# A two-block transformer on one core: four edits to the order of ACT, DVE and POOL, and scores of the compressed keys with the keys as weights

## The reference, cut to what matters

```python
h = x                                              # first block
h = h + moba_nsa_mixer(rmsnorm(h, mix_norm[0]))    # "even": 8 MoBA heads, 8 NSA heads
h = h + sqrelu_mlp(rmsnorm(h, mlp_norm[0]))        # "mlp0"
h = h + fox_mixer(rmsnorm(h, mix_norm[1]))         # "fox"
h = h + sqrelu_mlp(rmsnorm(h, mlp_norm[1]))        # "mlp1"
h = rmsnorm(h, final_norm)                         # the first block's last norm
# second block: n = rmsnorm(h) * g * (1 + scale) + shift, added back times a gate
h = h + 0.5 * gt1 * swiglu(n1)                     # "glu0"
h = h + gt2 * hybrid_mixer(n2)                     # "dil": pooling and dilated attention
h = h + 0.5 * gt3 * swiglu(n3)                     # "glu1"
out = rmsnorm(h, g_final)
```

```python
s_cmp = einsum('gjqd,gnd->gjqn', qn, k_cmp) * scale + bias
p_cmp = masked_softmax(s_cmp, d_cmp >= 0)
o_cmp = einsum('gjqn,gnd->gjqd', p_cmp, v_cmp)
```

## Time and profile before

| | us |
|---|---|
| median of 3 runs (lowest, highest) | 1099.05 (1098.44, 1100.7) |
| the profiled execution | 1098.95 |
| its span, first to last instruction | 1097.2 |
| busy in it: PE / PEld / DVE / ACT / POOL | 1076.2 / 918.3 / 778.6 / 660.4 / 115.5 |
| mean granted clock of PE | 0.996 |

### The profile page before, as it was taken

One profiled execution on the slowest core, in us unless ns is written; L12 is line 12 of the kernel. 1 busy time (PEld: TensorE's weight loads), 2 busy tenths in 40 slices (PEclk: granted clock), 3 DMA queues, 4 the chain that ended last, 5 costly groups with the idle time before them and its releaser, 6 DMA issues.

```text
span 1097.2 us, 15918 instructions
## 1 busy us (share of the span) xinstructions
PE 1076.2 (98%) x6098; PEld 918.3 (84%) x6098; DVE 778.6 (71%) x1261; ACT 660.4 (60%) x1067; POOL 115.5 (11%) x209
## 2 busy tenths in 40 slices
PE   8999999999999999999999999999999999999997
PEld 7898788888888998888888788888878978888885
DVE  6767667777786776687676777887875766565566
ACT  6667676565666776766565754354475766444443
POOL 2033101010100531020000000110000200000000
PEclk9999999999999999999999999999999999999999
DMA  9842348878864643687778467768545344555551
GB/s 341 298 158 79 115 156 326 304 289 306 300 217 173 212 140 113 217 306 279 255 277 312 154 227 289 294 244 312 188 165 183 131 154 173 192 191 183 185 183 64
DMA packets 40619, 238.30 MB, mean 217 GB/s; under 512 B 4661, under 2 KB 5845, under 8 KB 17632
## 3 DMA queue, kind: packets, MB, share of 16 engines
q1 hardware_dynamic: 26784, 188.81, 48.3%
q0 software_dynamic: 13040, 47.85, 11.7%
q10 hardware_dynamic: 720, 0.62, 0.2%
HBM read 236.15 MB, written 1.11 MB: 216 GB/s over the span
## 4 chain that ended last, share of the span: by engine, by line
PE 81%; DVE 9%; ACT 5%; issue 3%; DMA 1%; POOL 0%; DVEq 0%; ACTq 0%
PE bank L1570 20%; PE bank L1539 13%; PE bank L1541 13%; PE bank L1540 13%; PE bank L1571 10%; PE bank L1694 2%; DVE w_lo L1070 2%; PE bank L1758 1%; ACT w_hi L699 1%; PE bank L1740 1%; DVE ada_raw L1300 1%; PE bank L1732 1%; PE bank L1588 1%; PE bank L1589 1%; PE bank L1592 1%
## 5 line engine op out<-in xcount | busy, mean ns | idle before, releaser
L1570 PE MATMUL bank<-a_two,w_hi 128*128 128x512 f32 x1088 | 386.9, 399 | 0.8 <-DVE w_lo L1070 0.8
L1070 DVE TENSOR_TENSOR w_lo<-raw,w_hi 128x2048 fp32r<-128x2048 f32 x122 | 278.4, 2303 | 107.2 <-ACT w_hi L699 107.1
L1571 PE MATMUL bank<-a_two,w_lo 128*128 128x256 f32 x1088 | 305.5, 281 | 0.0
L699 ACT ACTIVATE w_hi<-raw 128x2048 fp32r<-128x2048 f32 x122 | 232.2, 1910 | 63.5 <-DMA raw<-in_stream 63.4
L1570 PEld LDWEIGHTS bank<-a_two,w_hi 128*128 128x128 f32 x1088 | 204.5, 188 | 51.0 <-issue 1.4
L1571 PEld LDWEIGHTS bank<-a_two,w_lo 128*128 128x128 f32 x1088 | 205.7, 189 | 1.7
L1539 PE MATMUL bank<-w_lo,hid_hi 128*128 128x512 f32 x432 | 169.6, 393 | 0.3 <-DVE w_lo L1070 0.2
L1540 PE MATMUL bank<-w_hi,hid_lo 128*128 128x512 f32 x432 | 168.7, 390 | 0.0
L1541 PE MATMUL bank<-w_hi,hid_hi 128*128 128x512 f32 x432 | 168.6, 390 | 0.0
L871 ACT ACTIVATE cross<-bank 128x256 f32<-128x256 f32 x136 | 51.5, 381 | 186.2 <-PE bank L1571 186.1
L1059 DVE TENSOR_TENSOR w_lo<-raw,w_hi 128x1024 fp32r<-128x1024 f32 x104 | 125.5, 1229 | 22.3 <-ACT w_hi L688 22.2
(11 more groups left out here) (231 smaller groups left out, 1478.4 us busy)
## 6 DMA issues: line engine op xcount, KB each, us to landing
raw<-in_stream SPq DMA_DIRECT2D x173, 1024.0 KB, 5.0
ada_raw<-in_ada POOLq DMA_DIRECT2D x72, 512.0 KB, 5.3
cmpw<-in_stream SPq DMA_DIRECT2D x4, 1024.0 KB, 8.1
rel_band<-rel_scratch POOLq DMA_DIRECT2D x2, 1024.0 KB, 7.2
cum_row<-cum_scratch POOLq DMA_DIRECT2D x4, 512.0 KB, 4.8
gate_row<-gate_scratch POOLq DMA_DIRECT2D x3, 512.0 KB, 5.8
h<-in_x SPq DMA_DIRECT2D x2, 512.0 KB, 4.3
raw<-in_stream SPq DMA_DIRECT2D x2, 512.0 KB, 7.0
```

Of the source, the lines that this page charges most:

```text
L699: nc.scalar.activation(w_hi[:, u % RING, :], raw[:, u % RING, :], ACT.Copy).then_inc(hi_ready, 2)
L1070: nc.vector.tensor_tensor(w_lo[:, u % RING, :], raw[:, u % RING, :], w_hi[:, u % RING, :].bitcast(F32), ALU.subtract).then_inc(lo_ready, 2)
L1570: nc.tensor.matmul(ps[bank][:, 0:2 * T], wh[:, k, cols_], a_two[:, :, k, :], start=k == 0, stop=False)
L1571: ins = nc.tensor.matmul(ps[bank][:, T:2 * T], wl[:, k, cols_], a_hi[:, k, :], start=False, stop=k == KT - 1)
```

## The change

- ACT, at the start: chunk 3 of both tiles and two halves of unit 3 are done before the copy of `rrow`. DVE's order there is not changed.
- POOL, at the start: the first zeroes wait until DVE has done six halves of `w_lo`.
- Even mixer: the scores of the compressed keys are made with `kc` as weights (128 x 32) and the queries of both token tiles (256 columns) as what moves, in plain fp32. The four heads of a group write to four groups of 32 partitions of bank 2. This is done one tick earlier, in km0/0. ACT copies the bank to the new buffer `score_rows`, and in km0/1 PE turns it with four transposes back to the layout that DVE reads.
- The turns `gmix` and `gf2` get a function of their own on ACT and DVE, `gated_turn`. ACT takes tile 1's root before chunk 3 of tile 0 and before the half unit. DVE shifts chunk 1 before chunk 0's low part, adds tile 1's second half before it shifts chunk 3, adds epsilon right after that, and makes the inverse before chunk 3's low part.
- glu0: the two halves of each tile of the first block's last norm are scaled in steps j and j + 1, not both in j.

```diff
@@ -263,6 +263,7 @@
 
         par = place("par", [P, N_COLS])
         kc = place("kc", [P, 2, 2, 16], F32R)
+        score_rows = place("score_rows", [P, 2, T])
         vcmp = place("vcmp", [16, 2, HD])
         four_rows = place("four_rows", [P, 32])
         hidc = place("hidc", [P, 2, 2, 32])
@@ -601,6 +604,7 @@
             pool.dma_start(rpick[:, :], rel_pick).then_inc(pick_landed, 16)
             pool.dma_start(bfor[:, :], b_forget).then_inc(bfor_landed, 16)
             pool.wait_ge(pool_step, 1)
+            pool.wait_ge(lo_ready, 6)
             zeros(slice(0, 6), 0)
             pool.wait_ge(rel_rows_sb, 1)
             pool.dma_start(rel_dram[:, 0:REL], rrow[:, :]).then_inc(rel_stored, 16)
@@ -764,6 +768,21 @@
                 inv = fin[:, t, 12:13] if name == "gf1" else stat[:, 7, t:t + 1]
                 for c0, c1 in ((0, 256), (256, 512), (512, 1024)):
                     nc.scalar.activation(tok[:, t, c0:c1], h[:, t, c0:c1], ACT.Copy, scale=inv).then_inc(rows_scaled_act, 1)
+
+            def gated_turn(name, gain, shift):
+
+                squares(name, 0)
+                round_half()
+                scale(name, 0)
+                turned(name, 0, gain, shift, (0, 1))
+                square_half(name, 1, 0)
+                turned(name, 0, gain, shift, (2,))
+                square_half(name, 1, 1)
+                root(name, 1)
+                turned(name, 0, gain, shift, (3,))
+                round_half()
+                scale(name, 1)
+                turned(name, 1, gain, shift)
 
             def norm_turn(name, gain, shift=None):
 
@@ -935,10 +954,12 @@
                 turned("mix0", t, gain0, chunks=(2,))
             round_half()
             round_half()
+            for t in range(TT):
+                turned("mix0", t, gain0, chunks=(3,))
+            round_half()
+            round_half()
             act.wait_ge(rel_rows, 1)
             nc.scalar.activation(rrow[:, :], ps[4][0:16, 0:REL], ACT.Copy).then_inc(rel_rows_sb, 1)
-            for t in range(TT):
-                turned("mix0", t, gain0, chunks=(3,))
             advance(FIRST["v_even"] + 4)
 
             def even_extras(tick):
@@ -963,6 +984,9 @@
                     act.wait_ge(ck_done, 1)
                     nc.scalar.activation(kc[:, :, 0, 0:15], ps[2][:, 0:32].rearrange("p (g n) -> p g n", g=2)[:, :, 0:15],
                                          ACT.Copy).then_inc(kc_hi, 1)
+                if tick.at("km0", 0, 0):
+                    act.wait_ge(crows, 1)
+                    nc.scalar.activation(score_rows[:, :, :], ps[2][:, :].rearrange("p (g t) -> p g t", g=2), ACT.Copy).then_inc(crows_sb, 1)
                 if tick.at("km1", 0, 0):
                     act.wait_ge(cshifted, 1)
                     nc.scalar.activation(pc[:, :, 0:15], pc[:, :, 0:15], ACT.Exp, scale=-1.0).then_inc(cprobs, 1)
@@ -998,7 +1022,7 @@
             act.wait_ge(gain_ready, 2)
             norm_turn("gf1", gainc[:, 0:KT], modc[:, 0:KT])
             glu("glu0")
-            norm_turn("gmix", gainc[:, KT:2 * KT], modc[:, 3 * KT:4 * KT])
+            gated_turn("gmix", gainc[:, KT:2 * KT], modc[:, 3 * KT:4 * KT])
             advance(FIRST["uv_dil"] + 4)
 
             def dil_extras(tick):
@@ -1025,7 +1049,7 @@
 
             mixer("dil", DIL_TICKS, dil_extras)
             act.wait_ge(gain_ready, 3)
-            norm_turn("gf2", gainc[:, 2 * KT:3 * KT], modc[:, 6 * KT:7 * KT])
+            gated_turn("gf2", gainc[:, 2 * KT:3 * KT], modc[:, 6 * KT:7 * KT])
             glu("glu1")
             for t in range(TT):
                 squares("last", t)
@@ -1086,12 +1110,16 @@
                     chain(nc.vector.tensor_tensor(tok[:, t, half], ps[bank][:, :], gate[:, half], ALU.mult))
                     nc.vector.tensor_tensor(to, to, tok[:, t, half], ALU.add).then_inc(h_ready, 1)
 
-            def inverse_root(name, t):
-
+            def first_mean(name, t):
+
+                dve.wait_ge(sumsq, squares_before(name, t) + 1)
+                nc.vector.tensor_scalar(stat[:, 2, t:t + 1], stat[:, 0, t:t + 1], EPS[name], None, ALU.add).then_inc(mean_ready, 1)
+
+            def inverse_root(name, t, first_taken=False):
                 n = NORM[name]
                 first, v, y, b = (stat[:, i, t:t + 1] for i in (2, 4, 5, 6))
-                dve.wait_ge(sumsq, squares_before(name, t) + 1)
-                nc.vector.tensor_scalar(first, stat[:, 0, t:t + 1], EPS[name], None, ALU.add).then_inc(mean_ready, 1)
+                if not first_taken:
+                    first_mean(name, t)
                 dve.wait_ge(mean_ready, n + t + 1)
                 dve.wait_ge(sumsq, squares_before(name, t) + 2)
                 chain(nc.vector.tensor_scalar(v, stat[:, 1, t:t + 1], first, -0.5, ALU.add, ALU.mult))
@@ -1150,20 +1178,23 @@
                 polish(t, 9, 11, 14, 15)
                 chain(nc.vector.scalar_tensor_tensor(out=f[:, 13:14], in0=f[:, 15:16], scalar=1.5, in1=f[:, 14:15], op0=ALU.add, op1=ALU.mult))
 
-            def turned(name, t, gain, shift=None, chunks=(0, 1, 2, 3)):
+            def shift_chunk(name, t, c, gain, shift):
 
                 m = TURN[name] + 4 * t
+                dve.wait_ge(bank_turned, m + c + 1)
+                if t == 1:
+                    dve.wait_ge(act_split, m - 4 + c + 1)
+                for kt in (2 * c, 2 * c + 1):
+                    ins = nc.vector.tensor_scalar(shifted[:, c, kt % 2, :], ps[TURN_BANKS[name][t][c]][:, (kt % 2) * P:(kt % 2 + 1) * P],
+                                                  gain[:, kt:kt + 1], shift[:, kt:kt + 1], ALU.mult, ALU.add)
+                ins.then_inc(rows_shifted, 1)
+
+            def turned(name, t, gain, shift=None, chunks=(0, 1, 2, 3), shifts=True):
+
                 ts = slice(t * P, (t + 1) * P)
                 for c in chunks:
-                    if shift is not None and c < 2:
-                        odd = 2 * c + 1
-                        dve.wait_ge(bank_turned, m + odd + 1)
-                        if t == 1:
-                            dve.wait_ge(act_split, m - 4 + odd + 1)
-                        for kt in (2 * odd, 2 * odd + 1):
-                            ins = nc.vector.tensor_scalar(shifted[:, odd, kt % 2, :], ps[TURN_BANKS[name][t][odd]][:, (kt % 2) * P:(kt % 2 + 1) * P],
-                                                          gain[:, kt:kt + 1], shift[:, kt:kt + 1], ALU.mult, ALU.add)
-                        ins.then_inc(rows_shifted, 1)
+                    if shift is not None and c < 2 and shifts:
+                        shift_chunk(name, t, 2 * c + 1, gain, shift)
                     dve.wait_ge(act_high, split_no(name, t, c))
                     bank, c0 = turned_at(name, t, c)
                     if shift is not None:
@@ -1177,6 +1208,24 @@
                                 out=a_lo[:, kt, ts], in0=ps[bank][:, c0 + (kt % 2) * P:c0 + (kt % 2 + 1) * P],
                                 scalar=gain[:, kt:kt + 1], in1=a_hi[:, kt, ts].bitcast(F32), op0=ALU.mult, op1=ALU.subtract)
                     ins.then_inc(act_split, 1)
+
+            def gated_turn(name, sums, gain, shift, gate):
+
+                for k in range(2):
+                    add(name, sums, gate, 0, k)
+                inverse_root(name, 0)
+                rest_half()
+                add(name, sums, gate, 1, 0)
+                shift_chunk(name, 0, 1, gain, shift)
+                turned(name, 0, gain, shift, (0, 1), False)
+                add(name, sums, gate, 1, 1)
+                shift_chunk(name, 0, 3, gain, shift)
+                first_mean(name, 1)
+                turned(name, 0, gain, shift, (2,))
+                inverse_root(name, 1, True)
+                turned(name, 0, gain, shift, (3,))
+                rest_half()
+                turned(name, 1, gain, shift)
 
             def norm_turn(name, sums, gain, shift=None, gate=None):
 
@@ -1272,12 +1321,11 @@
                 nc.vector.tensor_tensor(hid_lo[:, slot, :], hid_f[:, :], hid_hi[:, slot, :].bitcast(F32),
                                         ALU.subtract).then_inc(hid_ready, 1)
 
-            def last_norm(t):
-
-                for k in range(2):
-                    half = slice(512 * k, 512 * k + 512)
-                    nc.vector.scalar_tensor_tensor(out=h[:, t, half], in0=h[:, t, half], scalar=fin[:, t, 13:14], in1=row[:, half],
-                                                   op0=ALU.mult, op1=ALU.mult).then_inc(h_final, 1)
+            def last_norm(t, k):
+
+                half = slice(512 * k, 512 * k + 512)
+                nc.vector.scalar_tensor_tensor(out=h[:, t, half], in0=h[:, t, half], scalar=fin[:, t, 13:14], in1=row[:, half],
+                                               op0=ALU.mult, op1=ALU.mult).then_inc(h_final, 1)
 
             def gains(names):
 
@@ -1357,9 +1405,10 @@
                             modulation_column(p)
                         if (name, j) == ("glu0", FF2 - 2):
                             gains(("gf2",))
```

(29 more changed lines are left out.)

2 lines of the change are left out of this document (added).

## The result

The changed kernel takes 1092.11 us (median of 6 runs, 1091.45 to 1093.27); the kernel before, run 6 times with it, takes 1098.70. The ratio is 0.9941, with a 95% interval from 0.9928 to 0.9954: 6.6 us faster. Predicted were 1092.0 (range 1089.9 to 1096.0), with faster at 0.90. The profiled execution is the slowest of the six: 1093.27 us, with a span of 1091.5.

What follows compares the result with a forecast made beforehand. PE was taken as the bound, busy 1076.2 of 1097.2 us, so gains come from less PE work or idle time. Terms 0.7 + 1.0 + 1.6 + 0.3 + 1.0 + 1.2 + 1.1 = 6.9 off 1098.95 gave 1092.0, range 1089.9 to 1096.0.

Steps and rivals of the forecast that it cites:

- 1. Zeroes: Start: POOL's memsets moved later free DVE's slow scaling of the second tile; 0.7 us, bounds 0 and 0.67.
- Clock at the start: Start: PE's wait shrinks from 1.87 to about 1.2 us and the clock is kept; 1.0 us, bounds 0 and 1.2.
- 2. `rrow`'s order: Start: with `rrow` behind chunk 3 and unit 3, PE's wait for `w_lo` near 27 us goes whole; 1.6 us.
- 3. Scores: Even mixer: 16 matmuls (1.8 us) become 16 packed records (1.0) and four transposes (0.5); gain 0.3 us.
- 4. Gated turns: gmix and gf2: ACT scales 0.5 us sooner, PE's wait falls to 0.95 us; 1.0 us for two turns.
- Clock behind gf2: After gf2: with the wait at 0.95 us the clock is kept; 1.2 us, bounds 0 and 1.2.
- 5. The last norm: glu0: splitting the norm's halves over two units removes both PE waits for `w_lo`; 1.1 us, bounds 0.5 and 1.1.
- The falls of the clock stay or move: Rival on the clock: one more fall costs 1.0 to 1.2 us, both 2.2, giving 1093.0 to 1094.2; chance 0.27.
- Waits come back: Rival: waits return behind those removed, gated turns give nothing, clock falls at gf2; 1095.8, up to 1096.9 us; chance 0.11.
- The packed matmuls: Rival in the even mixer: the packed score matmuls run one after the other, 2.6 us more, 1094.6; chance 0.04.
- The slower case: Rival: the even mixer's PE, ACT, PE hand-over stops PE and drops the clock; eight falls give 1101.6 us; chance 0.02.
- signs of being wrong: Whole kernel: the clock falls as often as before, or PE's own waits do not shrink by about 4 us.

Runs made afterwards that it cites:

- run 6: Not a label: in "run 6 times with it" the kernel before was executed six times beside the changed kernel, taking 1098.70 us.
- the swap: Changed kernel with ACT's scaling of tile 1 ahead of its half-unit rounding in both gated turns: 1094.88 us, ratio 0.9973.
- the second set: Changed kernel with eight more fp32 matmuls of the same shape ahead of the packed eight, all written to partitions 0 to 31: 1097.39 us, one run.

## Why the prediction was right, and where it was not

The total came out 0.1 us off, which is better than its parts were, and that is luck: the turns were read 0.5 too small and the norm 0.4 to 0.5 too large, and the two falls of the clock are fewer only on the average over executions.

**1. Zeroes: right.** 0.7 predicted, 0.67 by the scaling's row (1155 to 488 ns at most) and 0.68 by the experiment that puts them back, counted from the first scaling. **Clock at the start: read low, and the reason not shown.** Kept, it gave 1.35 (1.0 predicted, 1.2 as the upper bound). The step said that the wait shrinks by the scaling alone, to about 1.2, and that the clock is kept for that. But the wait also depends on when PE is done with the first tile, and came out anywhere from 0.67 to 1.60 with the zeroes late; and the clock was kept after 1.60, and after 1.46 with the zeroes early. All twelve experiment kernels kept it there in their profiles; only the profile of before, with 1.87, lost it. That the length decides was not tried by itself, and stays open.

**2. `rrow`'s order: right.** 1.6 predicted, 1.66 measured; undone, the wait of 1.44 is back.

**3. Scores: right.** 0.3 predicted, 0.4 measured. The sixteen records took 1.07 us (1.0 from the earlier trace rows); the transposes cost 0.39 from start to start, where the step took the duration, 0.5. The copy ran when timed (75.8 less the 3.5 us that the kernel is ahead by, 72.4) and was covered.

**4. Gated turns: too small.** The step took the wait to 0.95 and had ACT scale at the end of a rounding that starts 0.66 after the root; by the rows the root (813.08) comes 0.82 after the squares start, as timed, but the rounding starts 0.51 after the root and the scaling follows 0.95 after that. The wait fell to 0.73, the gain was 0.73 and 0.77 in place of 0.5 each. That ACT would be last was right, and the swap shows why it must be. **Clock behind gf2:** kept in this profile, 1.36 against 1.2. It is kept in the old turns' profile too, behind a wait of 1.48, so the shorter wait did not have to do it.

**5. The last norm: too large.** 1.1 predicted, 0.6 to 0.7 measured. The failed step is "Both waits go". The one at 676 went. The one at 710 went from 0.36 to 0.25, and the pair put back leaves it at 0.28. The step held that the unit between has room for the moved half; it has none on DVE, and the half is still missing at the second root (687.40 and 704.86 above). Its price was also read high, from start to start, as 0.5 where the row says 0.36.

**What the prediction had as a rival.** "The falls of the clock stay or move" came half true in the profiled execution: two falls before, one after, at a third place, gf1. Take the clock out and the parts stand alone. Executions with a granted clock of 0.998 or 0.999 on the mean took 1091.45 to 1092.49 in the changed kernel (four of six, median 1091.73); of before, the nine such ones among the 52 runs beside the experiments took 1096.05 to 1097.81 (median 1096.33). That is 4.6 us, and the terms of the sum without the clock were 0.7 + 1.6 + 0.3 + 1.0 + 1.1 = 4.7. The remaining 2 us between the medians are then the clock's, about one and a half falls of 1.36 fewer, where the sum had 2.2 for two. The granted clocks fit this: the profiles show 0.998 or 0.999 without a fall, 0.996 or 0.997 with one and 0.994 to 0.996 with more, and the mean is 0.9957 over the 52 runs of before and 0.9980 over the six. So the clock's two terms are an average over executions and not two places won.

"Waits come back" had two small cases: 0.54 at 607, longer or shorter or absent by the execution, and 0.25 at 707, which is the case "the norm's pieces only move their waits" for one of the two. The packed matmuls did run beside each other; had they not, the second set prices it: 217 - 67 = 150 ns a record, 2.4 us for sixteen, near the 2.6 predicted. The slower case did not appear; PE never waited for ACT's copy. Of the signs of being wrong none came: PE's listed waits went from 13.4 to 9.3 us, but 0.7 of this is PE coming later to the second tile at the start.

## What to carry to other kernels

Where PE is busy for 98% of the span, list its idle gaps and ask of each what stands in the releasing engine's queue directly ahead of the releaser; here the edits of order and the packed scores gave 4.6 us. Ask also whether the step that takes over moved work has room for it: here DVE and ACT wait for each other in turn, and a delay of half a tile was handed on to the next root. Work taken out of the way must still be done before it is late: a filler behind the scaling cost more than it won, and the same filler ahead of the squares cost nothing where its data had landed, and gave back more than half of its gain where it had not. When parts are smaller than the spread of executions, read them at a fixed series of events along the kernel, count from the same first event (the input came up to 0.3 us apart here), and set the clock's falls apart before adding up.

## What the runs showed of the hardware that was not expected

- **A fall of the clock moves.** Of the fourteen profiles four had none before the kernel's end (old turns, old scores, last norm as a pair, early rounding in gf2), seven had one, six of these behind gf1 and one behind gf2, and three had two. The same program part, gf1 with its wait of about 1.53, kept the clock in the profile of before and lost it in that of the changed kernel. A fall at gf1 or gf2 cost 1.3 to 1.4 us in the ledger. The Trainium skill, TensorE: Matmul & The Clock Gate, section What's actually happening, has the watch free-running, and this agrees. The first rise moves too: PE's steps on zeroes went from 213 to 112 ns at 4.4 us in one execution and at 7.2 in another, and PE's wait ahead of the second tile was 1.60 and 0.67 us.
- **Column groups of the array overlap whatever the order.** Eight fp32 matmuls of 128*32 against 256 columns, sixteen records, took 1.07 us spread over four groups of 32 partitions, and 15 steps of 217 ns on one group: 3.2 times. With the two of a group next to each other it was 1.09.
- **A memset on POOL doubles DVE's time for one operation and not for another.** DVE's scaling of 128x512 went from 484 to 1158 ns beside it (zeroes early), and `w_lo`, from two inputs, took 2.29 us beside two of them, where 2.304 is its mean. The memset that started while a scaling ran (7.35 us in the earlier trace rows) left that scaling at its 0.48 and took 1.58 itself, against 1.38 and 1.39 late in the changed kernel. The Trainium skill, SBUF, section Who interferes with whom, has the second as a rule, and the row agrees.
